# A hybrid two-layer block on one core: the first two weight units and the gates fed with x before its inverse root

## The reference

```python
def _rmsnorm(x, w=None):
    y = x * lax.rsqrt(jnp.mean(x * x, axis=-1, keepdims=True) + 1e-6)
    return y if w is None else y * w

u = _rmsnorm(h, norm_w)                  # (1, 256, 2048), h = x
proj = jnp.matmul(u, w_in)               # 2048 x 20528: q, k, v, gates of an mLSTM; qkv, z, b, a of a gated delta net
qkv = _causal_conv_silu(dn_qkv, dn_conv_w)   # four taps along the tokens, then silu
i_pre = _softcap(ml_i + ml_i_bias); logf = log_sigmoid(_softcap(ml_f + ml_f_bias))
beta = sigmoid(dn_b); g = -exp(dn_a_log) * softplus(dn_a + dn_dt_bias)
```

## Time and profile before

| | |
|---|---|
| median of 3 runs | 1914.96 us (1913.67 to 1916.21) |
| span of the profiled execution, first to last instruction | 1913.3 us |
| PE busy | 1895.3 us, 99% of the span |
| DVE busy | 1398.8 us, 73% |
| ACT busy | 947.8 us, 50% |
| POOL busy | 344.2 us, 18% |

### The profile page before, as it was taken

One profiled execution on the slowest core, in us unless ns is written; L12 is line 12 of the kernel. 1 busy time (PEld: TensorE's weight loads), 2 busy tenths in 40 slices (PEclk: granted clock), 3 DMA queues, 4 the chain that ended last, 5 costly groups with the idle time before them and its releaser, 6 DMA issues.

```text
span 1913.3 us, 27611 instructions
## 1 busy us (share of the span) xinstructions
PE 1895.3 (99%) x10948; PEld 1638.9 (86%) x10948; DVE 1398.8 (73%) x1970; ACT 947.8 (50%) x1409; POOL 344.2 (18%) x543
## 2 busy tenths in 40 slices
PE   8999999999999999999999999999999999999998
PEld 8989999878888999988888888888888888888886
DVE  5686777676989888989989768665465686657675
ACT  6556566654544333444445465554444455544544
POOL 1025344351122222223223200000000000111000
PEclk9999999999999999999999999999999999999999
DMA  7455454555788877777888857755556543544563
GB/s 257 133 167 176 122 172 137 155 160 172 262 274 286 271 257 239 238 261 241 298 284 300 305 200 231 230 181 184 191 173 209 176 131 123 182 151 149 181 229 132
DMA packets 209744, 393.16 MB, mean 205 GB/s; under 512 B 13000, under 2 KB 62448, under 8 KB 208208
## 3 DMA queue, kind: packets, MB, share of 16 engines
q1 hardware_dynamic: 191248, 323.17, 51.6%
q0 software_dynamic: 18224, 68.17, 11.3%
q10 hardware_dynamic: 144, 0.07, 0.0%
HBM read 387.13 MB, written 4.23 MB: 205 GB/s over the span
## 4 chain that ended last, share of the span: by engine, by line
PE 94%; DVE 2%; ACT 2%; issue 1%; DMA 0%; SPq 0%; DVEq 0%; ACTq 0%
PE GB L2152 53%; PE GB L2179 18%; PE GB L2164 9%; PE GB L2167 5%; PE SB L415 1%; PE SB L1723 1%; PE SB L1715 1%; PE SB L819 1%; PE SB L784 1%; PE SB L1822 1%; PE SB L1829 1%; PE SB L1179 1%; ACT WH L2071 1%; DVE WL L2076 0%; DMA xin<-in_x 0%
## 5 line engine op out<-in xcount | busy, mean ns | idle before, releaser
L2076 DVE TENSOR_TENSOR WL<-raw,WH 128x1024 fp32r<-128x1024 f32 x605 | 732.3, 1237 | 197.4 <-ACT WH L2071 196.4
L2071 ACT ACTIVATE WH<-raw 128x1024 fp32r<-128x1024 f32 x605 | 621.7, 1057 | 320.5 <-PE GB L2152 227.1
L2152 PE MATMUL GB<-WH,uHL 128*128 128x512 f32 x1792 | 484.9, 392 | 0.0
L2152 PEld LDWEIGHTS GB<-WH,uHL 128*128 128x128 f32 x1792 | 333.3, 188 | 68.1 <-issue 0.5
L2179 PE MATMUL GB<-uHL,WH 128*128 128x256 f32 x2048 | 294.9, 287 | 1.6 <-DVE uHL L451 1.6
L2152 PE MATMUL GB<-WH,hHL 128*128 128x512 f32 x1024 | 279.5, 395 | 0.0
L2152 PE MATMUL GB<-WL,uHL 128*128 128x512 f32 x896 | 276.0, 389 | 0.0
L2179 PEld LDWEIGHTS GB<-uHL,WH 128*128 128x128 f32 x2048 | 265.6, 192 | 6.2 <-issue 3.4
L2152 PEld LDWEIGHTS GB<-WH,hHL 128*128 128x128 f32 x1024 | 190.6, 188 | 41.1 <-issue 2.7
L1409 DVE SCALAR_TENSOR_TENSOR macc<-wm,csil,macc 128x512 f32<-128x512 f32 x300 | 209.3, 745 | 2.8 <-DMA wm<-in_w_mod 1.7
L2152 PEld LDWEIGHTS GB<-WL,uHL 128*128 128x128 f32 x896 | 168.2, 188 | 35.4
(11 more groups left out here) (403 smaller groups left out, 1968.3 us busy)
## 6 DMA issues: line engine op xcount, KB each, us to landing
raw<-in_w_in SPq DMA_DIRECT2D x512, 512.0 KB, 4.6
raw<-in_w_out SPq DMA_DIRECT2D x96, 512.0 KB, 5.0
wm<-in_w_mod POOLq DMA_DIRECT2D x64, 512.0 KB, 5.5
wm<-in_w_mod POOLq DMA_DIRECT2D x64, 256.0 KB, 4.2
xin<-in_x SPq DMA_DIRECT2D x4, 512.0 KB, 5.7
E<-decay_rows POOLq DMA_DIRECT2D x4, 512.0 KB, 4.2
hres<-in_x POOLq DMA_DIRECT2D x1, 2048.0 KB, 10.8
cin<-in_ctx POOLq DMA_DIRECT2D x1, 2048.0 KB, 11.3
```

The costliest lines, as they stand in the source:

```text
L2071: e.activation(place(s)[0][:, :, :], raw[s % NR][:, :, :], ACT.Copy).then_inc(*wh.inc("WH", s))
L2076: e.tensor_tensor(low[:, :, :], raw[s % NR][:, :, :], f32(high[:, :, :]), sub).then_inc(*wl.inc("WL", s))
L2152: m = e.matmul(banks[j][:, :], x[:, c, 128 * j:128 * j + 128], w[:, k, :], start=i == 0 and k == 0 and n == 0, stop=i == 7 and k == 1 and ...
```

## The change

x is no longer scaled in place. PE transposes it as it comes, and the first two units (`RAW` = 2: slots 0 to 15) and the gates are multiplied with x without its inverse root. The roots become a row `rrow` (256 tokens, the same on all partitions) by one matmul of ones with two diagonal matrices (`norm_dve`, `norm_pe`, `norm_act`), whose steps stand at slots 2 to 7. `rrow` is applied behind the product: to the gates by one DVE instruction (`w`) at step 8, and to units 0 and 1 by four DVE instructions (`z`) from PSUM into the scratch `squares[1]`, from which ACT and DVE then take the taps. From slot 16 on the products need the scaled x, so a "rescale" replaces it block by block: POOL adds `uH` and `uL` and multiplies by `rrow` (two instructions of 128x512, eight times), ACT rounds, DVE subtracts; PE waits for block i before slot 16 + i. x arrives in eight column pieces (both row halves, 256 columns), issued by ACT with `ident` and `vcol`, while SP starts at once with the weights. Slot 0 has an order of its own (`first_pe`). `busy_pe` keeps its first 15 matmuls alone.

```diff
+RAW = 2
+NXA, NXD, NXP = (2, 3, 4, 5, 6, 7), (5.5, 6), (6.5,)
+FIRST_CONVS = (1, 1.5, 2, 3, 4, 5, 6, 10, 12, 13, 16)
+    at("nxa", 0, NXA)
+    at("nxd", 0, NXD)
+    at("nxp", 0, NXP)
+    for i in range(8):
+        at("rsp", 9 + i, (0,))
+        at("rsa", 11 + i, (0,))
+        at("rsd", 11 + i, (0.5,))
     at("gates", 0, GATES)
...
             e.tensor_scalar(rb[:, 0:1], rb[:, 0:1], 1.0 / 15.0, None, mul).then_inc(*g_dve.inc("rb"))
             yield
+            e.wait_ge(*g_pe.at("g"))
+            e.wait_ge(*nx_act.at("row"))
+            e.tensor_tensor(r(WW), SB[0][:, 0:256], rrow[:, :], mul).then_inc(*g_dve.inc("w"))
             yield
             e.wait_ge(*g_act.at("t"))
...
+        def norm_pe(e, bank):
+            e.wait_ge(*nx_dve.at("diag"))
+            claim(e, bank, 2, nx_act.at("row"))
+            m = e.matmul(SB[2][:, 0:256], ones[:, :], junk[:, 0:256], start=True, stop=True, skip_group_check=True)
+            m.then_inc(*nx_pe.inc("row"))
+            yield
...
+        def rescale_pool(e):
+            row = rrow[:, :].unsqueeze(1).to_broadcast([128, 2, 256])
+            for i in range(8):
+                k, scr = slice(2 * i, 2 * i + 2), halves_of[i % 2]
+                e.wait_ge(*slot.at("mm", 8 * RAW - 8 + i))
+                if i >= 2:
+                    e.wait_ge(*rs_dve.at("l", i - 2))
+                e.tensor_tensor(scr, f32(uH[:, k, :]), f32(uL[:, k, :]), add).then_inc(*rs_pool.inc("s", i))
+                if i == 0:
+                    e.wait_ge(*nx_act.at("row"))
+                e.wait_ge(*rs_pool.at("s", i))
+                e.tensor_tensor(scr, scr, row, mul).then_inc(*rs_pool.inc("r", i))
+                yield
+
+        def rescale_act(e):
+            for i in range(8):
+                e.wait_ge(*rs_pool.at("r", i))
+                e.activation(uH[:, 2 * i:2 * i + 2, :], halves_of[i % 2], ACT.Copy).then_inc(*rs_act.inc("h", i))
+                yield
+
+        def rescale_dve(e):
+            for i in range(8):
+                k = slice(2 * i, 2 * i + 2)
+                e.wait_ge(*rs_act.at("h", i))
+                e.tensor_tensor(uL[:, k, :], halves_of[i % 2], f32(uH[:, k, :]), sub).then_inc(*rs_dve.inc("l", i))
+                yield
...
@@ conv_dve
+            if r < RAW:
+                e.wait_ge(*slot.at("mm", end("qkv", r)))
+                e.wait_ge(*nx_act.at("row"))
+                for j in range(4):
+                    v = e.tensor_tensor(squares[1][:, j, :], half(banks[j // 2], j % 2), rrow[:, :], mul)
+                v.then_inc(*z_dve.inc("z", r))
+                yield
             yield
...
-                    e.scalar_tensor_tensor(out=y[:, j, sh:], in0=half(banks[j // 2], j % 2)[:, 0:256 - sh],
+                    p = squares[1][:, j, :] if r < RAW else half(banks[j // 2], j % 2)
+                    e.scalar_tensor_tensor(out=y[:, j, sh:], in0=p[:, 0:256 - sh],
...
@@ product_pe
+            if (unit.kind, unit.n) == ("qkv", RAW):
+                e.wait_ge(*rs_dve.at("l", i))
...
@@ block.scalar
-            e.dma_start(ident[:, :], A["c_ident"]).then_inc(ident_in, 16)
-            norm_act(e)
-            split_act(e, 0)
-            e.wait_ge(*nx_dve.at("rstd"))
-            scaled_act(e, "a")
-            scaled_act(e, "b")
+            for p in range(8):
+                if p == 1:
+                    e.dma_start(ident[:, :], A["c_ident"]).then_inc(ident_in, 16)
+                    e.dma_start(vcol[:, :], A["c_vcol"]).then_inc(vcol_in, 16)
+                e.dma_start(xin[:, :, 256 * p:256 * p + 256],
+                            x_rows[:, :, 256 * p:256 * p + 256]).then_inc(x_in[p], 16)
```

More of the change, by code:

```diff
@@ L640, in norm_act @@
         def norm_act(e):
[L641 to L646, removed]
+            for j in range(2):
+                for i in range(2):
+                    n = 2 * j + i
+                    for p in range(4):
+                        e.wait_ge(x_in[4 * j + p], 16)
                     if n >= 2:
                         e.wait_ge(*nx_act.at(f"s{n - 2}"))
-                    e.activation(s_junk[:, 1024 * j:1024 * j + 1024], xin[:, i, 1024 * j:1024 * j + 1024], ACT.Square,
-                                 accum_out=st[:, n:n + 1]).then_inc(*nx_act.inc(f"s{n}"))
+                    e.activation(s_junk[:, 1024 * i:1024 * i + 1024], xin[:, i, 1024 * j:1024 * j + 1024], ACT.Square,
+                                 accum_out=st[:, 2 * i + j:2 * i + j + 1]).then_inc(*nx_act.inc(f"s{n}"))
+                    yield
             e.wait_ge(*nx_dve.at("var"))
             e.activation(st[:, 4:6], rs[:, 0:2], ACT.Sqrt).then_inc(*nx_act.inc("sqrt"))
[L654 to L667, removed]
+            yield
+            e.wait_ge(*nx_pe.at("row"))
+            e.activation(rrow[:, :], SB[2][:, 0:256], ACT.Copy).then_inc(*nx_act.inc("row"))
+            yield
         def norm_dve(e):
@@ L718, in conv_act @@
             y, th = yth[:, 0], yth[:, 1]
-            e.wait_ge(*slot.at("mm", end("qkv", r)))
+            if r < RAW:
+                yield
+                e.wait_ge(*z_dve.at("z", r))
+            else:
+                e.wait_ge(*slot.at("mm", end("qkv", r)))
             if r == 0:
@@ L724, in conv_act @@
             for j in range(4):
-                a = e.activation(y[:, j, :], half(banks[j // 2], j % 2), ACT.Identity,
+                a = e.activation(y[:, j, :], squares[1][:, j, :] if r < RAW else half(banks[j // 2], j % 2), ACT.Identity,
                                  scale=col(CONV + 144 + 16 * kind + 4 * n + j), bias=0.0)
@@ L778, in conv_pe @@
                 m = 2 * n + kind
-                for _ in range(8):
+                for _ in range(9 if r < RAW else 8):
                     yield
@@ L792, in conv_pool @@
                 m = 2 * n + kind
-                for _ in range(9):
+                for _ in range(10 if r < RAW else 9):
                     yield
@@ L2136, in product_pe @@
             else:
[L2137 removed]
+                m = channels_pe(e, unit, s, banks, stages) if s else first_pe(e, banks)
             m.then_inc(*slot.inc("mm", s))
@@ L2168, in halves_pe, with first_pe @@
                                  skip_group_check=True)
+            return m
+        def first_pe(e, banks):
+            wh_, wl_ = place(0)
+            for said, x, w, ks in ((tr_act.at("h", TU), uH, wh_, (0, 1)), (tr_dve.at("l", TU), uL, wh_, (0, 1)),
+                                   (wl.at("WL", 0), uH, wl_, (0, 1))):
+                if w is wh_:
+                    e.wait_ge(*wh.at("WH", 0))
+                e.wait_ge(*said)
+                for k in ks:
+                    for j in range(4):
+                        m = e.matmul(half(banks[j // 2], j % 2), w[:, k, 128 * j:128 * j + 128], x[:, k, :],
+                                     start=x is uH and w is wh_ and k == 0 and j % 2 == 0, stop=False, skip_group_check=True)
             return m
```

76 lines of the change are left out of this document (46 added, 30 removed).

## The result

The changed kernel takes 1937.05 us (median of 4 runs, 1936.55 to 1937.38) against 1914.93 (4 runs of before beside them, 1913.67 to 1916.21): ratio 1.0119 with a 95% interval of 1.0104 to 1.0133, 22.1 us slower. The direction was forecast, the size was not: 1927.0 was the number and 1933 the end of the range. The profiled execution has 1937.38 us as its own time, beside a span of 1935.6, against 1913.3.

A forecast was written before the change was run, and what follows sets the result against it. PE was taken as the bound, busy 1895.3 of 1913.3 us. Holes of 19.4 less 6.0 gained gave +13.4, or +10.9 without the taps; +12 was taken: 1913.3 + 12 + 1.7 = 1927.0, range 1914 to 1933.

The forecast's parts named there:

- the sum up to G: Entrance: first product at 9.65 instead of 15.61; gate matmuls end (G) at 45.8, 6.0 us ahead of 51.77.
- so I take the full clock: Slot 0 and start of slot 1: full instead of half clock, 1.75 us more gained, less 0.2.
- The entrance does not gain: Rival: half clock and late pieces leave the gate matmuls' end only 3 us ahead; 1931 with full turns; chance 0.05.
- No term hangs on that: Entrance: x piece 1 might land at about 8.8, its transposes still ahead of ACT; given no size in the sum.
- The walk behind G: From the gate matmuls' end, G, to slot 24: it starts at G+64.7 instead of G+45.3, holes of 19.4 us.
- The turns: Rescale beside WL: POOL and DVE instructions go one after the other; full or nearly, 1923 to 1933, chance 0.51.
- With the taps taking part: Taps of units 0 and 1, reading `squares[1]`, also alternate with POOL: +13.4 us; without them +10.9.
- +12: Whole kernel: the net slowdown in us taken for the forecast, from sums of +13.4 and +10.9.
- No turns: Rival, rescale: POOL costs DVE nothing; holes 10.4, net +4.4, 1919.4; part or no turns (1917 to 1923) chance 0.23.
- The lead covers it: Rival, slots 16 to 24: splits stay ahead of PE, lateness below 5.0 us at slot 16; 1909; chance 0.13.
- Holes equal the gain: Rival: PE holes of 2 to 10 us give 1911 to 1919, no change or nearly; chance 0.08.

The follow-up runs named there:

- the experiment with fillers: Changed kernel with 13 and 5 small matmuls of ones on PE behind its first two pairs of transposes: 1934.75 us.
- w late: Changed kernel with DVE's `w` and its wait for the gate matmuls moved from step 8 to step 10: 1932.24 us.
- that last kernel: Changed kernel with entrance DMAs reordered, `w` at step 10, `z` written back in PSUM, taps read there, and later gate arithmetic moved behind the rescale: 1923.78 us.

## Why the prediction was wrong in size and right in kind

**The step that failed** is the sum up to G: "ACT issues ten DMAs at 0.41 = 4.1 us from 0.73, then a table load of 1.28, and is ready at 6.3", with "which hides the first x piece and `ident`" ahead of it and "so I take the full clock" behind it. Ten issues took 9.15 us, so ACT was ready at 11.3 and the first product started at 13.13 and not 9.65 (3.5 us); the second pair of transposes waited until 11.03, and PE's idle time ahead of the product put slot 0 on the half clock (5.49 in place of 2.88 + 0.2, 2.4 us; the experiment with fillers shows it). The rest, 0.6 us, was not taken apart. What held the issues, above all the last one with its 3.46 us, is open: SP's issues beside them or their own queue. I had this case as a rival, "The entrance does not gain", with 3 us left of the gain and a chance of 0.05. It was the case that came, and worse than I priced it. The evidence was thin: one issue of `ident` on a queue that was empty, 0.41 us, multiplied by ten, although SP's issues in the same stretch would run beside them. Of the landing of x piece 1 I had written "No term hangs on that". One did, the full clock: PE idled 3.03 us for this piece. And the order of bytes, which had no term, decides once ACT is free of the issues: with x on SP's queue the weights of slot 4 come too late, and the forecast G comes out when the order is changed as well.

**The walk behind G held in its mechanism; that its end came out so well is partly luck.** Slot 24 at G+64.7 forecast, G+65.4 measured. The kinds of wait are as I put them: DVE's wait at step 8 (6.65 us), WL above 2 us beside POOL (twice), holes in front of slots 16, 17, 19, 20 and 24. Two places are not: there is a hole of 0.82 in front of 18 and none in front of 23. The 20.1 us are 15.2 of holes, some 4 of half clock in slots 19 and 20, and 0.9 that is neither. On the way two errors cancel. WL of slot 16 ends at G+22.7, where I had G+24.4, because it came ahead of POOL and POOL paid; WL of 19, 20 and 23 are 1.2 to 1.7 early as well. Then the taps behind WL 23, priced at 1.4, take 3.66 beside L860, and WL of slot 24 ends at G+65.2, 0.5 late. POOL's product for q and k was a term at nothing, 2.2 us. The turns are shown by the durations above, which are gone where POOL's instructions are short (10.0 us less), and for the taps by reading one input from PSUM (1.51 in place of 3.47). With the taps taking part the forecast was +13.4, without them +10.9. The Trainium skill, GPSIMD Engine Reference, "Key points", says that POOL shares its SBUF interfaces with DVE and contends with DVE instructions that have two SBUF inputs; the trace agrees (3.47 against 1.51).

**A term was left out**: the half clock behind a hole. The hole in front of slot 24 is followed by a granted 0.5 to 0.6 up to 122, with no later hole in which that could vanish: 1.7 us. Of it 1.6 is slot 24 itself, 4.44 from its start to that of slot 25. My sum counted a hole by its length only. And I took +12 between 10.9 and 13.4, 1.4 us under what the full walk gave.

Together: 13.4 + 6.5 (entrance) + 0.7 (walk) + 1.7 (clock) = 22.3, the difference of the spans.

**The rivals.** No turns: ruled out by the two experiments just named. The lead covers it: ruled out, the lead is gone at slot 16 (a hole of 2.35 there); with w late there is no hole at 16, and still 3.9 and 4.2 at 19 and 20. Holes equal the gain: they are 15.2 us, and there was no gain for them to equal. The hole in front of slot 19 belongs to the gate arithmetic with its logarithm: it is 0.37 once they stand later. Open is how much of the 2.5 us left in front of slot 20 is POOL's and how much that of `l` and z of unit 1; these were not taken apart in that kernel.

## What to carry to other kernels

Taking a row scaling off the entrance and applying it behind the product moves work from where the critical engine is not running yet to where it has no slack: find the lead of the helpers at the place where the deferred work lands (5 us here), and compare it with the sum of that work, counting POOL's and DVE's times added where both read two tiles in SBUF, and with other POOL work that the delay brings beside DVE's (L860 here). At an entrance list the bytes in the order in which they are wanted, over all queues, constants too; here a second queue, issued from ACT beside SP's, gave neither early data nor a free engine. After a hole count the clock too.

## What the runs showed of the hardware

- The eight issues of x on ACT took a median of 0.63 us and up to 3.46 while SP's queue was fetching 512 KB blocks beside them; before, with one issue on ACT, it was 0.41. ACT's next work, the table load, starts at 9.91, right behind the last issue.
- POOL's 128x512 instructions take 1.30 us alone and up to 2.35 beside a DVE instruction with two SBUF inputs; WL takes 1.22 alone and up to 2.31 beside them. Which of the two pays is a matter of which started first: at 73.81 it is POOL, at 81.50 DVE. Taps with one input in PSUM are not touched (1.51).
- The granted clock fell behind some holes and not behind others, and their length alone does not say which: behind 2.35 us in front of slot 16 eight matmuls take 1.19 us at the full clock, behind 2.40 us in front of slot 24 it is 0.59, and with POOL's work made tiny a hole of 3.35 us in front of slot 24 is followed by 1.19 again.
- A DVE instruction with a single small SBUF input waits for POOL as well: L575 (128x32) took 1.26 us beside POOL's 2.35 and ended with it, at 76.2, and where the gate arithmetic stands behind the rescale the same instruction takes 0.17. Timeline of DVE in that last kernel:

```profile
87.51 0.17 DVE L575 TENSOR_SCALAR colBe<-colBe 128x32 f32<-128x32 f32 x1
```
